# A PEER expert layer on one core: v rows gathered and summed half a block behind u, in halves of the experts

## The reference

```python
def peer_ffn(h, w_query, sub_keys, u_table, v_table):
    ...
    q = (hf @ w_query).reshape(-1, PEER_HEADS, 2, PEER_HALF)
    s = jnp.einsum('nhpk,hpmk->nhpm', q.astype(jnp.float32), sub_keys.astype(jnp.float32))
    sv, si = lax.top_k(s, PEER_TOPK)
    comb = (sv[:, :, 0, :, None] + sv[:, :, 1, None, :]).reshape(-1, PEER_HEADS, PEER_TOPK * PEER_TOPK)
    ...
    fv, fpos = lax.top_k(comb, PEER_TOPK)
    eid = jnp.take_along_axis(cidx, fpos, axis=-1)
    gate = jax.nn.softmax(fv, axis=-1).astype(h.dtype)
    ...
        a = jnp.einsum('phkd,pd->phk', u_table[ex], hx)
        act = jax.nn.gelu(a, approximate=False) * gx
        return jnp.einsum('phk,phkd->pd', act, v_table[ex])
```

```python
    h1 = rmsnorm(x, g_norm1) * (1 + sc1) + sh1
    mix, new_pool, new_conv = token_mixer(h1, ...)
    x = x + gt1 * mix
    h2 = rmsnorm(x, g_norm2) * (1 + sc2) + sh2
    x = x + gt2 * peer_ffn(h2, w_query, sub_keys, u_table, v_table)
```

## Time and profile before

| | us |
|---|---|
| median of 3 runs | 3320.57 |
| lowest and highest | 3314.8 and 3324.29 |
| the profiled execution | 3321.2 |
| its span in the trace | 3319.4 |

### The profile page before, as it was taken

One profiled execution on the slowest core, in us unless ns is written; L12 is line 12 of the kernel. 1 busy time (PEld: TensorE's weight loads), 2 busy tenths in 40 slices (PEclk: granted clock), 3 DMA queues, 4 the chain that ended last, 5 costly groups with the idle time before them and its releaser, 6 DMA issues.

```text
span 3319.4 us, 30349 instructions
## 1 busy us (share of the span) xinstructions
PE 2172.9 (65%) x9719; PEld 962.3 (29%) x9719; DVE 2132.8 (64%) x4860; ACT 360.3 (11%) x754; POOL 2284.6 (69%) x2229
## 2 busy tenths in 40 slices
PE   7884966567675588987564876674454445545576
PEld 5573532134331134542111443341111111111111
DVE  1577885767888557655756678777766666675301
ACT  2112340000001101321000000000000000000000
POOL 0144657677777777777767777777777777777675
PEclk9997988778887799999777887887666776786799
DMA  8778779999999999999999999999999999999998
GB/s 289 200 276 288 279 255 379 399 401 386 381 400 395 385 402 407 409 392 391 400 391 387 402 387 367 386 362 378 398 409 406 409 388 406 403 408 370 373 408 329
DMA packets 363454, 1235.06 MB, mean 372 GB/s; under 512 B 36856, under 2 KB 40336, under 8 KB 363280
## 3 DMA queue, kind: packets, MB, share of 16 engines
q0 software_dynamic: 304784, 1109.40, 86.7%
q1 hardware_dynamic: 36335, 79.69, 6.9%
q10 hardware_dynamic: 22176, 44.04, 3.5%
HBM read 1220.31 MB, written 13.28 MB: 372 GB/s over the span
## 4 chain that ended last, share of the span: by engine, by line
POOL 31%; DMA 26%; PE 22%; issue 11%; DVE 7%; DVEq 1%; ACT 1%; SPq 0%; POOLq 0%; ACTq 0%
DMA v_ring<-in_v_table_dram,eidt 19%; POOL u_ring L783 16%; POOL v_ring L800 14%; PE bank L1701 12%; DMA u_ring<-in_u_table_dram,eid 3%; PE bank L1520 3%; DVE u_ring L1337 2%; PE bank L1619 2%; PE bank L1537 2%; PE bank L1595 2%; DMA u_ring<-in_v_table_dram,eidt 1%; POOL u_ring L800 1%; DVE mixt L1176 1%; DMA wring<-in_w_in_dram 1%; DMA u_ring<-in_w_ada_dram 0%
## 5 line engine op out<-in xcount | busy, mean ns | idle before, releaser
L1701 PE MATMUL bank<-v_ring,act_x 128*32 128x512 f32 x3984 | 1165.9, 810 | 918.1 <-DMA v_ring<-in_v_table_dram,eidt 910.5
L1337 DVE CUSTOM_DVE_ANT_0 u_ring<-u_ring,h 128x1024 f32<-128x1024 f32 x1056 | 1278.4, 1225 | 745.3 <-DMA u_ring<-in_u_table_dram,eid 674.1
L783 POOL DMA_INDIRECT u_ring<-in_u_table_dram,eid x1024 | 1132.9, 1106 | 465.3 <-issue 302.8
L800 POOL DMA_INDIRECT v_ring<-in_v_table_dram,eidt x996 | 1041.4, 1046 | 392.0 <-issue 244.2
L1701 PEld LDWEIGHTS bank<-v_ring,act_x 128*32 128x32 f32 x3984 | 268.5, 135 | 1735.1 <-issue 1720.3
L1619 PEld LDWEIGHTS bank<-hbuf,wring 128*128 128x128 f32 x1984 | 230.1, 196 | 24.9 <-issue 24.9
L1619 PE MATMUL bank<-hbuf,wring 128*128 128x128 f32 (+1 forms) x1984 | 236.3, 280 | 0.0
L1537 PE MATMUL bank<-zc,dring 128*128 128x384 f32 x496 | 189.5, 508 | 7.7 <-ACT dring L832 7.7
L1520 PE MATMUL bank<-hbuf,wring 128*128 128x384 f32 (+2 forms) x448 | 151.4, 497 | 17.7 <-DMA wring<-in_w_in_dram 13.5
L1595 PE MATMUL bank<-wring,mixt 128*128 128x512 f32 (+1 forms) x256 | 125.0, 638 | 0.0
L1361 DVE TENSOR_TENSOR scratch<-bank,mod 128x512 f32<-128x512 f32 x18 | 11.6, 686 | 176.1 <-PE bank L1701 174.6
(11 more groups left out here) (260 smaller groups left out, 1679.6 us busy)
## 6 DMA issues: line engine op xcount, KB each, us to landing
u_ring<-in_u_table_dram,eid POOLq DMA_INDIRECT x1024, 7.1
wring<-in_w_out_dram ACTq DMA_DIRECT2D x16, 1024.0 KB, 11.7
wring<-in_w_query_dram ACTq DMA_DIRECT2D x16, 1024.0 KB, 11.6
v_ring<-in_v_table_dram,eidt POOLq DMA_INDIRECT x996, 7.5
wring<-in_w_in_dram ACTq DMA_DIRECT2D x10, 1024.0 KB, 11.7
xr<-in_x_prompt_dram SPq DMA_DIRECT2D x16, 512.0 KB, 7.3
v_ring<-in_w_ada_dram SPq DMA_DIRECT2D x7, 1024.0 KB, 13.5
wring<-in_w_ada_dram SPq DMA_DIRECT2D x5, 1024.0 KB, 5.4
```

Source lines behind the costliest of these rows:

```text
L783: pool.indirect_dma_start(u_ring[:, n % NU], None, u_table[0], bass.IndirectOffsetOnAxis(ap=col, axis=0)).then_inc(u_in[n % NU], 16)
L800: pool.indirect_dma_start(place, None, v_table[0], bass.IndirectOffsetOnAxis(ap=eidt[:, b % RING, t:t + 1], axis=0)).then_inc(landed, 16)
L1337: dve.tensor_tensor_reduce(u_ring[:, n % NU], u_ring[:, n % NU], h2[:, b % 2], 1.0, 0.0, ALU.mult, ALU.add, dot[:, b % 2, k:k + 1]).then_i ...
L1701: last = pe.matmul(acc[h][j * S:(j + 1) * S, :], act_x[:, i % 2, j, a:a + S], v_place(n)[0][:, h * HALF:(h + 1) * HALF], start=(c == 0), s ...
```

## The change

v now runs half a block behind u. The unit of the v side is half a block's experts: as soon as the first 64 experts of each token (heads 0 to 3) have their dot products, their v rows are gathered, in chunks 16 to 31 of the same pass; the second 64 follow in chunks 0 to 15 of the next pass (`LAG`, `v_chunk`). A gather now brings 64 experts of one token on the lower 64 partitions and the same 64 experts of another token on the upper 64. The weights and the numbers are turned by halves to fit: TensorE transposes 64 columns twice, onto the lower and the upper partitions, and copies of 64 partitions each take the right tokens from the two (`numbers`, `weights`, `transposed_numbers`, `spread`). A product's weight matrix has two columns that aren't zero, 16 apart, each on its own half of the partitions. The number of gathers, of products and their shapes stay the same.

`finish` of a block moves from the start to the middle of the pass behind, with its loads and stores of y. Weighting, turning, taking and spreading are done at the middle and at the start of each pass. The v gather number 4 waits until VectorE has read block 0's scores. In `lay_out` group 1 starts at slot 2, the room is 8 up to slot 15 and then 6.6 and 6.4, and what a slot has over its room is carried to the next. Cut to what matters:

```diff
+LAG = NCH // 2
...
+HK2 = H * K // 2
...
-ROOM = [None, 4.8, 4.6]
+ROOM = [None, 6.6, 6.4]
...
-        last = [w[1] for w in was if w[0] == PARTS - 1]
-        out += [("turn", b) for b in last] + [("top", *x, i) for i in range(3, PIECES)] + [("turned", b) for b in last]
+        half = [(w[1], w[0] // 2) for w in was if w[0] % 2 and w != (1, SB)]
+        out += [("turn", *h) for h in half] + [("top", *x, 3)] + [("turned", *h) for h in half] + [("top", *x, 4), ("top", *x, 5)]
     b = todo[-1][1]
-    return out + [("gap", 1), ("exp", *todo[-1]), ("turn", b), ("gap", 1), ("nrm", *todo[-1]), ("gap", 1), ("turned", b)]
+    return out + [("gap", 1), ("exp", *todo[-1]), ("turn", b, 1), ("gap", 1), ("nrm", *todo[-1]), ("gap", 1), ("turned", b, 1)]
...
-            while load[at] >= (room if at >= NCH else 8):
+            while load[at] >= (room if at >= LAG else 8):
+                load[at + 1] += load[at] - (room if at >= LAG else 8)
                 at += 1
...
             last = int(at)
+            if i[0] == "turn" and last % LAG > LAG - 5:
+
+                last = at = last // LAG * LAG + LAG
...
-    at = 5
+    at = 2
...
-        SPREAD_AT = (0, 1, 10, 18)
-
-        turned = [sum(1 for s_ in range((p + 1) * NCH) for step in steps[s_] if step[0] == "turn") for p in range(NB + 1)]
+        SPREAD_AT = (0, 1)
+
+        turned = [sum(1 for s_ in range(LAG * (i + 1)) for step in steps[s_] if step[0] == "turn") for i in range(2 * NB)]
+        turned.append(2 * NB + 1)
+
+        def halves(s):
+
+            return min(s // LAG, 2 * NB)
+
+        def v_chunk(s):
+
+            return divmod(s - LAG, NCH) if 0 <= s - LAG < NB * NCH else None
...
-        V_LAST, U_ALL = LAST * P + CH * (NSG + 2), NB * P + NSG * CH
+        V_LAST, U_ALL = LAST * P + CH * (LAG + NSG + 1), NB * P + NSG * CH
...
-                if s % NCH == 3 and p >= 2:
-                    y_store(p - 2)
-                    y_load(p - 1)
+                if s % NCH == LAG + 3 and 0 < p < NB:
+                    y_store(p - 1)
+                    y_load(p)
...
-                    pool.wait_ge(eidt_ready, b + 1)
+                h, pair_no = divmod(i, HK2)
+                if pair_no == 0:
+                    pool.wait_ge(eidt_ready, 2 * b + h + 1)
                 if n == 0:
                     pool.wait_ge(mod_ps, 2 * 12)
+                if n == 4:
+                    pool.wait_ge(s0_used, 1)
...
-                t = S * (i % 4) + i // 4 if b < NB else i
+                t = HK2 * h + 16 * (pair_no % 4) + pair_no // 4 if b < NB else i
...
-                    for j in range(CH):
-                        if p:
-                            v_fetch(p - 1, c * CH + j)
-                    if p == 0 and c == NCH // 2:
+                    if v_chunk(p * NCH + c):
+                        b, vc = v_chunk(p * NCH + c)
+                        for j in range(CH):
+                            v_fetch(b, vc * CH + j)
+                    if p == 0 and c == LAG - 3:
...
+            def take_weights(b, h):
+                i = 2 * b + h
+                act.wait_ge(act_ps, i + 1)
+                if i:
+                    act.wait_ge(x_ready, 2 * i)
...
+                spots = act_x[:, i % 2, :, XB:XB + 8 * S].rearrange("p j (r c) -> p j r c", c=S)
                 if b < NB:
-                    src = actt[:, :].rearrange("p (j r) -> p j r", j=4)[:, :, 8 * i:8 * i + 8]
+                    src = actt[:, :].rearrange("p (j a q) -> p j a q", j=4, a=2)[:, :, :, 8 * (i % 2):8 * (i % 2) + 8]
+                    act.activation(spots[0:HK2, :, :, 0], src[0:HK2, :, 0], ACT.Copy)
+                    act.activation(spots[HK2:P, :, :, 16], src[HK2:P, :, 1], ACT.Copy).then_inc(x_ready, 1)
...
+                    if (part, b) == (PARTS - 1, 0):
+                        dve.drain().then_inc(s0_used, 1)
...
+            def transposed_numbers(b, h):
+
+                if b < NB:
+                    dve.wait_ge(eidt_ps, 2 * b + h + 1)
+                    to = eidt[:, b % RING, h * HK2:(h + 1) * HK2].rearrange("p (j q) -> p j q", j=4)
+                    src = ps[6][:, 0:P].rearrange("p (j a q) -> p j a q", j=4, a=2)
+                    dve.tensor_copy(to[0:HK2], src[0:HK2, :, 0])
+                    dve.tensor_copy(to[HK2:P], src[HK2:P, :, 1]).then_inc(eidt_ready, 1)
...
-                    dve.wait_ge(gel_ready, PARTS * (b + 1))
-                    dve.tensor_tensor(act_w[:, :], dot[:, b % 2], gate[:, b % RING].rearrange("p h k -> p (h k)"), ALU.mult)
+                    dve.wait_ge(gel_ready, PARTS * b + 2 * h + 2)
+                    if b:
+                        dve.wait_ge(act_ps, 2 * b + h - 1)
+                    where = slice(h * HK2, (h + 1) * HK2)
+                    dve.tensor_tensor(act_w[:, where], dot[:, b % 2, where],
+                                      gate[:, b % RING, h * H // 2:(h + 1) * H // 2].rearrange("p h k -> p (h k)"), ALU.mult)
...
-                        weigh(p - 1)
-                    if p > 1 and c == 0:
-                        finish(p - 2)
+                        weigh(p - 1, 1)
+                    if p < NB and c == LAG:
+                        weigh(p, 0)
+                    if p and c == LAG:
+                        finish(p - 1)
...
-            finish(LAST)
...
+                    for a in range(2):
+                        last = pe.matmul(ps[6][a * HK2:(a + 1) * HK2, 0:P], eidf[:, b % 3, h * HK2:(h + 1) * HK2], ident[:, :], start=True, stop=True)
...
-                    pe.transpose(ps[6][:, P:2 * P], act_w[:, :], ident[:, :]).then_inc(act_ps, 1)
+                    for a in range(2):
+                        last = pe.matmul(ps[6][a * HK2:(a + 1) * HK2, P:2 * P], act_w[:, h * HK2:(h + 1) * HK2], ident[:, :], start=True, stop=True)
+                    last.then_inc(act_ps, 1)
...
-                a = XB + 31 * r - 8 * i
+                a = XB + 31 * r - 8 * (i % 2)
...
-                    if p:
-                        if c == 0:
-                            weights(p - 1)
-                        tokens(p - 1, c)
+                    if v_chunk(p * NCH + c):
+                        b, vc = v_chunk(p * NCH + c)
+                        if vc % LAG == 0:
+                            weights(b, vc // LAG)
+                        tokens(b, vc)
+                    if p == NB and c == NSG + 2:
+                        weights(NB, 0)
```

82 lines of the change are left out of this document (40 added, 42 removed).

## The result

Four runs of the changed kernel have a median of 3351.8 us (3345.2 to 3354.6), four of the kernel before beside them 3321.3 us (3314.8 to 3324.3). The ratio is 1.0092, with a 95% interval of 1.007 to 1.0113: slower, by some 30 us, where I had forecast 17 us less. 3351.8 us also lies outside my range, which ended at 3340. Medians and ratios leave out two executions in a slow state, one of e7 (4700 us) and one of e13 (7892 us).

A forecast was written before the change was run, and what follows sets the result against it. Bound: a stream of row gathers, GpSimd's issue loop and DMA engines full together. 227.3 us saved less 190 (mixed half), 7 (x rows), 13 (hand-overs) gives 17.3 off 3320.6: 3303 us, 8-in-10 range 3268 to 3340.

The forecast's parts named there:

- The mixed half: Pass 0's second half, with 64 u and 64 v gathers after the change: 173 + 8 + 9 = 190 us.
- the two waits: Added to the mixed half: 8 us for block 0's first weights, 9 us for block 1's numbers at pass 1's start.
- Rival (b): Mixed half: gather issues stay long, 128 take 207 us, so the fill gains nothing; 3320 us, chance 0.24.
- The tail: Pass 8's v-only second half, block 7's last 64 v gathers running alone, is gone: 79.5 us saved.
- The x rows: Pass 0's first half: VectorE waits for block 4's x, normalised earlier; 7 us added, bounds 0 and 15.
- the gather that I gave as the sign: GpSimd's gather starting at 271.86 us before; would come 7 to 12 us late if the x term held.
- The hand-overs: Seven added starts of v rows at passes 2 to 8, 1.84 us each: 13 us, bounds 0 and 58.
- the old kind: Hand-overs with a block's finish beside them; claimed to move from the starts to the middle of passes.
- the quiet row: Pass 6's clean hand-over in the earlier trace: TensorE waits 7.05 us, GpSimd 1.84 us; the latter priced all seven.
- Rival (c): Each added hand-over costs 8.25 us like pass 5's, 58 instead of 13 us: 3348 us; with its kin, chance 0.18.
- the model of a full stream: Stretch 1265 to 1438 us, convolution beside both streams: 129 gathers in 173 us, taken for the mixed half.

The follow-up runs named there:

- e7: Changed kernel with the rooms of the kernel before (4.8, 4.6, no carry) from slot 16 and VectorE's product of dots and gates ahead of sorting: 3340.2 us, 1.0059.
- e13: Changed kernel with the whole planner of the kernel before and the product of dots and gates ahead of sorting, slower-gather chip: 3511.6 us, 0.9945.
- e1: Changed kernel with pass 0's steps on x rows of blocks 2 to 4 and input products three slots later: 3344.4 us, 1.0073.
- e14: Changed kernel with the whole planner of the kernel before (start slot 5, rooms 4.8 and 4.6), slower-gather chip: 3513.7 us, 0.9955.

## Why the prediction was wrong, by its steps

- **The mixed half, 190 us: right, with some luck.** 193.8 us, of which the two waits are 15 and the rest 179 for my 173. I had left the planner out, and it takes load from this half: with the steps three slots later (e1) it lasted 207.4 us. The first hand-over of block 0 showed a v row's wait of 9.6 us for my 8, the start of pass 1 waited 5.34 us for my 9. Rival (b), long issues through the half, fell: GpSimd was busy 135.70 us for 128 gathers, 1.06 us each, and 13 were longer than 1.5 us where 24 of 64 had been. The Trainium skill, "SBUF — State Buffer", section "Who interferes with whom", says that a VectorE instruction with two SBUF inputs contends with a GpSimd instruction that reads SBUF. The trace agrees: of this half's 59 issues beside no dot product 1 was longer than 1.5 us, of the 44 beside two or three 11. That v issues fall between the bursts of dot products, and so thin this out, is my reading.
- **The tail, -79.5 us: right**, at -84.4.
- **The x rows, +7 us: the step failed.** It measured +21.9, and the gather that I gave as the sign came at 291.65 us, 19.8 late and not 7 to 12. I counted the norms of blocks 2 and 3, which move ahead as well, as 5.5 us of work and no wait, took block 4's x buffer for the limit and bounded the term at 15 us; the limit was ScalarE's in-order queue under the norm of block 2 (20.18 us at 256.79). Put back, it gave 20.4 us in its half and 7 in the time.
- **The hand-overs, 7 x 1.84 = 13 us: mis-sized, 24 us.** The first v row's wait for products behind each hand-over shows it. At mid-pass, in passes 1 to 7, these waits sum to 15 us, as those of the kernel before do (15): the old kind did only move. The seven at the starts of passes 2 to 8 are 7.09, 1.70, 5.22, 6.54, 2.81, 0.94 and 0 us, 24 for my 13. I took the price of the quiet row for seven places, some of which stand beside the mixer. Two of my readings of the earlier trace rows were wrong as well: 6.15 and 2.95 us are waits of the 15th v row of their block, 45 us and more into the pass, and no hand-over's; at pass 4's hand-over there was none, at pass 7's 1.56 us. Moving the product ahead of the sorting took 28 us back. Rival (c) gave 3348 us from 8.25 us each, 45 us over the forecast, where its own mechanism has some 11 to show: that its sum came out near is luck, next point.
- **The planner was missing from the sum.** The prediction counted the moved start once (x rows) and put the new rooms at nothing without a reason; the diff showed them. In the kernel before they and the start cost 26 us, 20 of them in one half of pass 3 that I had used as the model of a full stream; in the changed kernel the old order is worth 1.5%. No rival named it. The forecast's gain, 17.3 us or 0.52%, is near what the shift gives without it (0.9955 and 0.9952), but that is a likeness of sums: the x term is gone with start 5, the mixed half took 213.5 us in e14 for my 190, and no trace of the kernel before from those chips shows the other terms.
